# First attention's projections with tokens in the partitions, and the values' copy moved in the recurrence

## What is computed

```python
def first_block(x, norm1_g, w_in, q_norm_g, k_norm_g, rel_bias, ...):
    h = rms_norm(x, norm1_g)
    proj = jnp.einsum('bsd,de->bse', h, w_in)
    q, k, v, bg, cg, xc = jnp.split(proj, [...], axis=-1)
    # 16 heads of 64; q and k are divided by the root of their head's mean square
    q = rms_norm(q.reshape(b, nc, CHUNK, N_HEADS, HEAD_DIM), q_norm_g)
    k = rms_norm(k.reshape(b, nc, CHUNK, N_HEADS, HEAD_DIM), k_norm_g)

def gla_chunked(q, k, v, log_f):
    b = jnp.cumsum(log_f, axis=2)
    b_end = b[:, :, -1:]
    q_dec, k_dec, k_end = q * jnp.exp(b), k * jnp.exp(-b), k * jnp.exp(b_end - b)
```

## Time and profile before

| | |
|---|---|
| median of 3 runs (lowest, highest) | 2638.17 us (2632.98, 2641.39) |
| profiled execution: time, span | 2636.76 us, 2635.0 us |
| busy: TensorE, VectorE, GpSimd, ScalarE | 94%, 63%, 52%, 18% of the span |
| chain that ended last: TensorE, VectorE, ScalarE | 78%, 18%, 2% |
| mean granted clock of TensorE | 0.972 |

### The profile page before, as it was taken

One profiled execution on the slowest core, in us unless ns is written; L12 is line 12 of the kernel. 1 busy time (PEld: TensorE's weight loads), 2 busy tenths in 40 slices (PEclk: granted clock), 3 DMA queues, 4 the chain that ended last, 5 costly groups with the idle time before them and its releaser, 6 DMA issues.

```text
span 2635.0 us, 32100 instructions
## 1 busy us (share of the span) xinstructions
PE 2485.9 (94%) x12340; PEld 2019.5 (77%) x12340; DVE 1651.5 (63%) x2144; ACT 481.8 (18%) x1015; POOL 1370.3 (52%) x773
## 2 busy tenths in 40 slices
PE   7989999999999999888989999989899988999997
PEld 5767778887788876677768888868778876788885
DVE  7847764325904326577469994165788883899913
ACT  2103321000000000245210000023445431100000
POOL 6544446665656664344346666634243434466661
PEclk9989999999999999989999999989899999999998
DMA  4222222223222222112122222312111211232231
GB/s 148 80 72 89 85 76 96 96 97 104 88 96 96 96 89 72 64 57 65 59 70 96 96 96 96 97 55 73 40 65 57 65 48 64 67 100 98 96 96 56
DMA packets 59755, 214.58 MB, mean 81 GB/s; under 512 B 6624, under 2 KB 6752, under 8 KB 59488
## 3 DMA queue, kind: packets, MB, share of 16 engines
q1 hardware_dynamic: 56880, 206.68, 23.7%
q10 hardware_dynamic: 2736, 5.96, 0.7%
HBM read 210.51 MB, written 2.10 MB: 81 GB/s over the span
## 4 chain that ended last, share of the span: by engine, by line
PE 78%; DVE 18%; ACT 2%; issue 2%; DMA 0%; DVEq 0%; SPq 0%; ACTq 0%
PE acc L491 22%; PE acc L493 22%; PE acc L492 22%; PE ps_s L613 2%; DVE rstd L1215 2%; PE ps_o L635 2%; PE ps_t L570 2%; PE ps_t L623 2%; DVE u_hi L1203 1%; PE ps_s L836 1%; DVE hg_level_k L1697 1%; DVE hg_in L1649 1%; DVE hg_level_q L1697 1%; DVE u_tmp L1476 1%; DVE u_lo L1205 1%
## 5 line engine op out<-in xcount | busy, mean ns | idle before, releaser
L449 POOL CAST w_hi<-w_raw 128x1024 fp32r<-128x1024 f32 x384 | 413.3, 1076 | 1186.5 <-DMA w_raw<-stream 1186.5
L452 POOL TENSOR_TENSOR w_lo<-w_raw,w_hi 128x1024 fp32r<-128x1024 f32 x384 | 957.1, 2493 | 30.7
L491 PE MATMUL acc<-h_hi,w_hi 128*128 128x512 f32 (+1 forms) x2144 | 868.3, 405 | 29.8 <-DVE h_lo L1209 24.6
L493 PE MATMUL acc<-h_hi,w_lo 128*128 128x512 f32 (+1 forms) x2144 | 829.2, 387 | 0.0
L492 PE MATMUL acc<-h_lo,w_hi 128*128 128x512 f32 (+1 forms) x2144 | 827.5, 386 | 0.0
L491 PEld LDWEIGHTS acc<-h_hi,w_hi 128*128 128x128 f32 x2144 | 407.9, 190 | 126.9 <-DVE h_lo L1209 31.4
L492 PEld LDWEIGHTS acc<-h_lo,w_hi 128*128 128x128 f32 x2144 | 407.9, 190 | 88.2 <-issue 13.4
L493 PEld LDWEIGHTS acc<-h_hi,w_lo 128*128 128x128 f32 x2144 | 406.3, 189 | 82.7
L1246 DVE COPY y_all<-acc 128x512 f32<-128x512 f32 x32 | 22.1, 692 | 213.4 <-PE acc L493 212.0
L947 ACT ACTIVATE square<-x_res 128x512 f32<-128x512 f32 x48 | 30.3, 633 | 609.7 <-DVE x_res L1482 273.8
L493 PE MATMUL acc<-hid_hi,w_lo 128*128 128x512 f32 x352 | 137.0, 389 | 0.0
(11 more groups left out here) (252 smaller groups left out, 3456.0 us busy)
## 6 DMA issues: line engine op xcount, KB each, us to landing
w_raw<-stream SPq DMA_DIRECT2D x384, 512.0 KB, 3.3
toeplitz<-ext_in ACTq DMA_DIRECT2D x16, 256.0 KB, 3.7
out<-x_res SPq DMA_DIRECT2D x4, 512.0 KB, 2.7
x_res<-x_in SPq DMA_DIRECT2D x3, 512.0 KB, 6.8
mem<-mem_in ACTq DMA_DIRECT2D x1, 1024.0 KB, 4.8
consts<-consts_in SPq DMA_DIRECT2D x1, 784.0 KB, 9.8
x_res<-x_in SPq DMA_DIRECT2D x2, 256.0 KB, 5.1
rope<-rope_in ACTq DMA_DIRECT2D x1, 512.0 KB, 5.7
```

Of the source, the lines that this page charges most:

```text
L449: nc.gpsimd.tensor_copy(hi, raw).then_inc(hi_made, 1)
L452: nc.gpsimd.tensor_tensor(lo, raw, f32(hi), ALU.subtract).then_inc(split_made, 1)
L491: nc.tensor.matmul(ps, hi, x_hi[:, k, 0:cols], start=(k == 0), stop=False)
L493: mm = nc.tensor.matmul(ps, lo, x_hi[:, k, 0:cols], start=False, stop=(k == st.kt - 1))
```

## The change

**First part.** The stage `qkv` becomes six groups of four column blocks (q0, q1, k0, k1, v0, v1). In each the input tile (128 features x 128 tokens) is stationary and four weight tiles, 512 output columns, move through, so that an item is 128 tokens x 512 columns in one bank: 24 items. `TOKEN_BANKS` rotates them over seven banks (acc, ps_s, ps_o). The weight slots keep their layout and number. ScalarE makes h_hi (a copy with a factor), and VectorE only h_lo. The RMS of the tokens is turned into the partitions once (`rms_turned`). For each query or key item ScalarE squares, VectorE sums each head's 64 columns (reduction to 128 x 8), ScalarE takes eight roots per partition, VectorE inverts them and multiplies the bank into `qk_tok`, TensorE turns it (four transposes) during the next group, and ScalarE copies it to `qk` with the gain. Values are copied by ScalarE with a factor per partition, without a transpose. The attention's first two pairs of scores are computed within the last group.

**Second part.** In the recurrence ScalarE copies the values after the forward direction's exponentials instead of after the backward direction's. The index `v0` follows the smaller number of transposes.

```diff
 
+        TOKEN_BANKS = [0, 1, 2, 3, 4, 5, 6, 0, 1, 2, 3, 4, 5, 6, 0, 1, 2, 3, 4, 5, 0, 1, 2, 3]
+        token_bank = [[*acc, *ps_s, ps_o][i] for i in TOKEN_BANKS]
+
+        def token_free(i):
+
+            before = [j for j in range(i) if TOKEN_BANKS[j] == TOKEN_BANKS[i]]
+            return (stages[TOKENS[before[-1] // BLOCKS]].free, before[-1] % BLOCKS + 1) if before else None
+
...
+                    if units is units1 and j == 0:
+                        pe.wait_ge(stages["v1"].free, BLOCKS)
...
+                for j in range(begun, LOOK):
+                    scores(units, j)
...
-            lead(st, h_hi, h_lo, waits_for(h_ready, 0), first_norm)
+            def tokens(g, x_hi, x_lo, ready, then):
+
+                st = stages[TOKENS[g]]
+                for s in range(st.slots):
+                    slot = st.first_slot + s
+                    pe.wait_ge(split_made, slot + 1)
+                    for b in range(BLOCKS):
+                        i, cols = g * BLOCKS + b, slice(b * P, (b + 1) * P)
+                        if s == 0 and token_free(i) is not None:
+                            pe.wait_ge(*token_free(i))
+                        for half in range(2):
+                            k = 2 * s + half
+                            if ready is not None and b == 0:
+                                ready(k)
+                            hi, lo = (w[:, slot % RING, BANKS * half:BANKS * (half + 1), :].rearrange("p t n -> p (t n)")
+                                      for w in (w_hi, w_lo))
+                            out_ = token_bank[i][:]
+                            nc.tensor.matmul(out_, x_hi[:, k, cols], hi, start=(k == 0), stop=False)
+                            nc.tensor.matmul(out_, x_lo[:, k, cols], hi, start=False, stop=False)
+                            mm = nc.tensor.matmul(out_, x_hi[:, k, cols], lo, start=False, stop=(k == st.kt - 1))
+                        if b == BLOCKS - 1:
+                            mm.then_inc(slot_done, 1)
+                        elif s == st.slots - 1:
+                            mm.then_inc(tok_made, 1)
+                        then(s * BLOCKS + b)
+
+            def first_sums(at):
+
+                for i in {3: [0, 1], 7: [2, 3, 4], 11: [5, 6, 7]}.get(at, []):
+                    if i == 0:
+                        pe.wait_ge(small_in, 16)
+                    sum_square(i, DT, const("ones"))
+                if at == 13:
+                    take_t(rms_tok_made, 1)
+                    pe.wait_ge(rms_ready, 1)
+                    for b in range(BLOCKS):
+                        mm = nc.tensor.transpose(ps_t[:, b * P:(b + 1) * P], rms[:, b * P:(b + 1) * P], const("ident"))
+                    mm.then_inc(rms_turned, 1)
+
+            def turn_tokens(g, at):
+
+                if at in (2, 4, 6, 8):
+                    b = at // 2 - 1
+                    i = g * BLOCKS + b
+                    take_t(qk_ready, i + 1)
+                    pe.wait_ge(stages[TOKENS[g]].free, b + 1)
+                    for c in range(BANKS):
+                        cols = slice(c * P, (c + 1) * P)
+                        mm = nc.tensor.transpose(ps_t[:, cols], qk_tok[:, i % 2, cols], const("ident"))
+                    mm.then_inc(qk_turned, 1)
+
+            def first_scores(at):
+
+                if at in (3, 7):
+                    pe.wait_ge(qk_ready, 4 * BLOCKS)
+                    pe.wait_ge(stages["v0"].free, BLOCKS)
+                    scores(units1, at // 4)
+
+            tokens(0, h_hi, h_lo, waits_for(h_ready, 0), first_sums)
             n["h"] += DT
-            plan = lagged(st.cbs, BANKS, 2 * DT)
-            for c in range(BANKS, st.cbs):
-                block_at(st, c, h_hi, h_lo)
-                for i in plan[c]:
-                    sum_square(0, 1, const("pair_ones"))
-                if c > 2 * DT:
-                    transpose_v(st, c - 1, v_feat[:, (c - 1) % 2, :])
-            transpose_v(st, st.cbs - 1, v_feat[:, (st.cbs - 1) % 2, :])
-            pe.wait_ge(v_ready, n["v"])
-            pe.wait_ge(qk_ready, 2 * DT)
+            for g in range(1, 5):
+                tokens(g, h_hi, h_lo, None, lambda at, g=g: turn_tokens(g - 1, at))
+            tokens(5, h_hi, h_lo, None, first_scores)
...
+            nc.scalar.activation(small["head_root"][:, 0:1], small["eps_d"][:], ACT.Square)
             for part, (first, end) in enumerate(zip(X_CUTS[:-1], X_CUTS[1:])):
                 act.wait_ge(x_loaded[part], 16)
+                if part == 0:
+                    act.wait_ge(params_loaded, 16)
                 for i in range(first, end):
+                    nc.scalar.activation(h_hi[:, i, :], x_res[:, i, :], ACT.Copy, scale=param("norm1_g", i)).then_inc(x_hi_made, 1)
                     squared(x_res[:, i, :])
             root(DT, 1.0 / D, small["eps_d"][:])
-            st = stages["qkv"]
-            for c in range(2 * DT + 1):
-                if c < 2 * DT:
-
-                    act.wait_ge(st.free, c + 1)
-                    squared(qk[:, c, :])
-                if c:
-
-                    root(DT + c, 1.0, small["eps_q"][:])
+
+            def tok_squares(i):
+
+                act.wait_ge(*token_made(i))
+                if i >= 2:
+                    act.wait_ge(tok_sum, i - 1)
+                nc.scalar.activation(square[:, i % 2, :], token_bank[i][:], ACT.Square).then_inc(tok_square, 1)
+
+            def tok_roots(i):
+
+                cols = slice(8 * (i % 2), 8 * (i % 2) + 8)
+                act.wait_ge(tok_sum, i + 1)
+                act.wait_ge(rms_tok_made, 2)
+                nc.scalar.activation(small["head_root"][:, cols], small["head_sums"][:, cols], ACT.Sqrt,
+                                     bias=small["eps_tok"][:, i % BLOCKS:i % BLOCKS + 1]).then_inc(tok_root, 1)
+
+            def take_tokens(i):
+
+                g, b = divmod(i, BLOCKS)
+                act.wait_ge(qk_turned, i + 1)
+                nc.scalar.activation(qk[:, BANKS * g:BANKS * (g + 1), b * P:(b + 1) * P], ps_t[:].rearrange("p (c n) -> p c n", n=P),
+                                     ACT.Copy, scale=param("q_g") if g < 2 else small["k_g8"][:]).then_inc(qk_ready, 1)
+
+            def take_values(g):
+
+                for b in range(BLOCKS):
+                    act.wait_ge(*token_made(BLOCKS * g + b))
+                    nc.scalar.activation(v_tok1[:, b, T * (g - 4):T * (g - 3)], token_bank[BLOCKS * g + b][:], ACT.Copy,
+                                         scale=small["rstd_tok"][:, b:b + 1]).then_inc(stages[TOKENS[g]].free, 1)
+
+            for g in range(4):
+                first = BLOCKS * g
+                tok_squares(first)
+                for b in range(1, BLOCKS):
+                    tok_squares(first + b)
+                    tok_roots(first + b - 1)
+                tok_roots(first + BLOCKS - 1)
+                for b in range(BLOCKS):
+                    take_tokens(first + b)
+            take_values(4)
 
             act.wait_ge(setup_done, 2)
             nc.scalar.activation(small["lb_exp"][:], small["lb_exp"][:], ACT.Exp).then_inc(setup_act, 1)
-            attention(units1, probs, probs_t, {})
+            attention(units1, probs, probs_t, {}, lambda: take_values(5))
...
+            def head_rest(h, d):
+
+                act.wait_ge(hg_rest, 2 * h + d + 1)
+                end, near, rest = (end_f, end_b)[d][:, 1:CHUNKS + 1], (near_f, near_b)[d][:], hg_in[h % 2][:, 2 + d, :]
+                nc.scalar.activation(small["decay_" + "fb"[d]][:], end, ACT.Exp)
+                nc.scalar.activation(near, near, ACT.Exp)
+                nc.scalar.activation(rest, rest, ACT.Exp).then_inc(hg_rest_exp, 1)
 
             act.wait_ge(forget_made, 1)
             head_in(0)
@@ -1165,18 +1282,13 @@
                     b_ = hg_in[h % 2][:, 2 + d, :]
                     nc.scalar.activation(qd[:], b_, ACT.Exp).then_inc(hg_exp, 1)
                     nc.scalar.activation(grow[:], b_, ACT.Exp, scale=-1.0).then_inc(hg_exp, 1)
-                for d, way in enumerate("fb"):
-
-                    act.wait_ge(hg_rest, 2 * h + d + 1)
-                    end, near, rest = (end_f, end_b)[d][:, 1:CHUNKS + 1], (near_f, near_b)[d][:], hg_in[h % 2][:, 2 + d, :]
-                    nc.scalar.activation(small["decay_" + way][:], end, ACT.Exp)
-                    nc.scalar.activation(near, near, ACT.Exp)
-                    nc.scalar.activation(rest, rest, ACT.Exp).then_inc(hg_rest_exp, 1)
+                head_rest(h, 0)
                 if h:
                     head_square(h - 1)
 
                 act.wait_ge(vt_done, v0 + h + 1)
                 nc.scalar.activation(hg_v[:].rearrange("p b n -> p (b n)"), ps_t[:], ACT.Copy).then_inc(v_ready, 1)
+                head_rest(h, 1)
...
+                for i in range(first, end):
+                    dve.wait_ge(x_hi_made, i + 1)
+                    step.wait()
```

(60 more changed lines are left out.)

67 lines of the change are left out of this document (38 added, 29 removed).

## The result

| | before | changed |
|---|---|---|
| median (lowest, highest) | 2635.99 us (2632.98, 2641.39) | 2620.52 us (2615.31, 2622.79) |
| profiled execution: time, span | 2636.76, 2635.0 us | 2615.31, 2613.5 us |
| busy: TensorE, VectorE, GpSimd, ScalarE | 94%, 63%, 52%, 18% | 95%, 60%, 52%, 19% |
| mean granted clock | 0.972 | 0.974 |

The ratio is 0.9936, 95% interval 0.9913 to 0.996: 15.5 us faster by the medians, where 30 were forecast. The time lies 3.5 us above the range. The profiled execution of the changed kernel is the fastest of its four and 21.5 us shorter in span than that of before, so that its profile shows some 6 us more gain than the medians do.

What follows compares the result with a forecast made beforehand. VectorE's reciprocals were taken to bound the query and key projection, the VectorE-ScalarE loop the recurrence. Gains of 29.1 and 1.0 us, together 30.1, from 2636.76 gave 2606.7, stated as 2606.5 us; range 2597 to 2617, chance 0.80.

Steps and rivals of the forecast that it cites:

- Start and stalls: Projection's first group: TensorE starts at 9.1 us, then stalls behind h_lo of 2 and 1 us.
- cold start: Projection's first matmuls, run at low clock: 1.7 us extra.
- at half clock: Old projection: the first twelve matmuls ran at half clock, 4.41 us, 1.7 more than later ones.
- The sum of the first part: Projection to attention: first convolution matmul at 162.4 us, 27.6 us earlier; with the seam's clock 29.1.
- the clock at the seam: Seam from projection to attention: TensorE comes without a gap, so the low clock goes, 1.5 us more gain.
- The reduction: VectorE's sum per query or key item in the projection: between 0.69 and 3.35 us, taken as 0.7.
- the rival of handshakes: Projection items paced by handshakes between engines: 0.8 us at each of 16 turns, 13 us, time 2620; chance 0.08.
- The rival of bank cycling: Projection's rotation of PSUM banks; the prediction as given lists no such rival, size or chance.
- Bounds: 0 and 14.9. I take 1.0: Recurrence: gain from moving the values' copy, between 0 and 14.9 us, taken as 1.0.
- That loop passes TensorE by: Recurrence: the VectorE-ScalarE loop from scan to logarithm does not involve TensorE, so removing TensorE's wait makes VectorE no earlier.
- Sum. 29.1 + 1.0: Whole kernel: both parts' gains add to 30.1 us, with no loss expected in the attention.
- closer scans: Recurrence: scans expected still 43 to 45 us apart; moving closer together would show the forecast wrong.

Runs made afterwards that it cites:

- full: The changed kernel, both parts, run once more on the same chip as its two parts: 2619.48 us, ratio 0.9929 to before.
- hi_before_squares: Changed kernel with ScalarE making all eight h_hi ahead of the squares of tiles 2 to 7: 2616.46 us, ratio 0.9915 to before.
- second_alone: Kernel before with only the second part, the values' copy between forward and backward exponentials: 2643.57 us, ratio 1.0028 to before.
- the gate: GpSimd's fourth split per head waits for VectorE's next backward forget gate, one late split for the output gate; on the changed kernel 2606.69 us, before 2632.99.
- first_alone: Changed kernel without the second part, the values' copy back behind both directions' exponentials: 2616.72 us, ratio 0.9916 to before.
- no_low_before: Kernel before, GpSimd writing zeros instead of subtracting for the low parts of 40 weight slots in the recurrence: 2615.76 us, ratio 0.9920 to before.
- misgated_full: Changed kernel with the fourth split held to a wrong place, until the next head's first scan is done: 2619.86 us, ratio 0.9922 to before.

## Why the prediction was wrong

The forecast was 30.1 us; 15.5 came in the first measurement and 17.2 in full. On the chip of full, 9.1 us are missing from the first part (29.1 said, 20.0 measured), and the second part, said to give 1.0, costs 6.9 alone and 2.8 on top of the first. The smaller of the two shortfalls is explained, the larger one only located.

- **Start and stalls: right in mechanism.** TensorE started at 9.32 (9.1 was said); stalls of 2 and 1 us were said, 0.56 and 1.68 came. The cold start was taken too small: in the changed kernel the first twelve matmuls took 5.23 us (9.32 to 14.55) where twelve later ones take 2.73, so 2.5 us and not 1.7. The sentence on the first twelve of before "at half clock" misreads the row as well: only seven of them started at the slow pace of 0.43 us, though their excess of 1.7 us is right. hi_before_squares shows that the cause named, h_hi queued behind a waiting square, was the cause.
- **The sum of the first part: right.** 27.6 us earlier at the first convolution matmul, measured 27.0; with the clock at the seam 29.1, measured 28.6. The reduction took 686 ns where 0.69 to 3.35 us was the range and 0.7 was taken. No wait at the turns: the rival of handshakes found its time (2620) and not its mechanism. The rival of bank cycling did not come either: from 14.55 us on the matmuls start 0.23 us apart and the granted clock was 1.00. The Trainium skill, "TensorE: Matmul & The Clock Gate", section "A second HAM failure mode: psum-queue depth-cycling", tells of micro-idles between groups of matmuls, in which the clock swings, when the banks are cycled each iteration; with six matmuls per bank these rows show none.
- **What failed, first: the price of the second part, "Bounds: 0 and 14.9. I take 1.0".** The lower bound was wrong. "That loop passes TensorE by" was right as far as waits go, but the loop is tied to TensorE by another way: TensorE frees weight slots, a slot's release sets when GpSimd splits the next, and a split holds up VectorE, which is on the loop. The part costs 6.9 us alone (second_alone), nothing without the subtractions, and with the gate it costs nothing that shows. The hold was in the rows read: 2.74 us against 0.75 for h_lo. It was priced at the start of the kernel and never asked for in the recurrence, where VectorE sets the pace.
- **What failed, second: the sum carried the 29.1 us of 200 us unchanged to the end ("Sum. 29.1 + 1.0").** By the medians the first part gives 20.0. The profile of first_alone, whose execution is the slowest of its six, shows where its lead goes: 27.3 us at the first convolution matmul and at the first windowed query, 24.0 at the first hidden block of the feed-forward, 21.9 at the first scan and 17.7 at the last. So about 3 us go at the attention's end, 2 before the recurrence and 4 within it. The loss at the attention's end differs between executions of one program: full's lead falls from 31.6 us at the first windowed query (1009.48 before, 977.85) to 25.9 at the first hidden block (1378.30, 1352.38), and in the changed kernel's first profile it only goes from 29.4 to 28.7 there (980.11 and 1349.57). It goes with the clock: low-clock time between 1000 and 1390 us (about 28 us earlier in the changed kernels) is 17.2 us before, 17.0 in the first profile, 20.4 in first_alone and 22.2 in full. It is not shown that the clock is its cause, and no run was made on it. What widens first_alone's scans by 4.2 us is not shown either: its fourth splits lie where they should, and VectorE is busy only 1.4 us longer there than before. This part stays open.
- **What would prove it wrong** were closer scans; farther ones were not thought of, though they were the sign to look for.

## What to carry to other kernels

Before removing a wait, ask what else follows the freed engine's pace: a transfer or a split that starts on its release moves too, and if it shares a resource with the engine that sets the pace, a lower bound of zero is not safe. Look at where a background job falls between that engine's instructions, and where it happens to fall into a wait, tie it there by a semaphore. Here the gate gained 12.8 us on the changed kernel, 5.3 of them in a place that the change had not touched. And read a lead at several milestones down to the end, in more than one execution.

## What was not expected of the hardware

- Beside a GpSimd subtraction of 1024 columns (2.4 us when it is not held itself), a VectorE instruction on 128x4 numbers took 2.23 us instead of 0.17. Over the recurrence, putting shorter writes in place of 40 of them brings the scans 22.5 us closer together (308.2 to 285.7) and gives 22 us of time (no_low_before).
- GpSimd is held in turn: in misgated_full its cast took 2.03 us beside VectorE's scan instead of 1.04.
- Two executions of one program, the changed kernel, had low-clock time of 17.0 and 22.2 us in the same stretch of 390 us.
